# The first RMS norm of a hybrid decoder step moved into the first projection's block, and the squares of all four norms added on VectorE

## The reference

```
def rmsnorm(x, g):
    xf = xf * lax.rsqrt(jnp.mean(xf * xf, axis=-1, keepdims=True) + NORM_EPS)
    return xf * g

h = rmsnorm(x, norm_mix); z = h @ w_in           # then attention and RWKV branches on z
x = x + mixed @ w_out
h = rmsnorm(x, norm_mlp); x = x + square(relu(h @ w_ff1)) @ w_ff2
h = rmsnorm(x, norm_ple); x = x + sigmoid(h @ w_ple_gate) * (p @ w_ple)
y = rmsnorm(x, norm_final)
```

## Time and profile before

| | |
|---|---|
| time, median of 3 runs | 3305.36 us (3301.95 to 3306.35) |
| the profiled execution's own time | 3305.41 us |
| its span, first to last instruction | 3303.6 us |
| TensorE busy | 2969.5 us (90%) |
| VectorE busy | 1090.3 us (33%) |
| ScalarE busy | 954.6 us (29%) |
| mean granted TensorE clock | 0.935 |

### The profile page before, as it was taken

One profiled execution on the slowest core, in us unless ns is written; L12 is line 12 of the kernel. 1 busy time (PEld: TensorE's weight loads), 2 busy tenths in 40 slices (PEclk: granted clock), 3 DMA queues, 4 the chain that ended last, 5 costly groups with the idle time before them and its releaser, 6 DMA issues. The chain is left out here.

```text
span 3303.6 us, 62866 instructions
## 1 busy us (share of the span) xinstructions
PE 2969.5 (90%) x27318; PEld 2390.3 (72%) x27318; DVE 1090.3 (33%) x2430; ACT 954.6 (29%) x1797; POOL 407.5 (12%) x398
## 2 busy tenths in 40 slices
PE   6888797889999999999987999988999999999797
PEld 3666676856666666666655666687999999999785
DVE  1120202216777777777762111013111111111222
ACT  2120202025555555555542000013122221222212
POOL 0000001002111111112110000011221212212010
PEclk8889796599999999999988999999999999999898
DMA  3211102210001001001001110020111111111011
GB/s 135 80 61 58 70 14 78 105 27 23 25 11 33 19 17 33 19 17 33 13 3 47 42 41 30 12 103 26 45 38 44 44 38 44 38 44 44 29 40 61
DMA packets 57474, 139.18 MB, mean 42 GB/s; under 512 B 5008, under 2 KB 37008, under 8 KB 52400
## 3 DMA queue, kind: packets, MB, share of 16 engines
q1 hardware_dynamic: 53376, 116.03, 10.4%
q10 hardware_dynamic: 3888, 20.05, 1.8%
HBM read 119.54 MB, written 16.54 MB: 41 GB/s over the span
## 5 line engine op out<-in xcount | busy, mean ns | idle before, releaser
L1535 PE MATMUL psum<-hT,rkv_w 128*64 128x256 f32 (+1 forms) x3072 | 412.3, 395 | 11.2 <-DMA rkv_w<-in_w_pair 9.9
L1535 PEld LDWEIGHTS psum<-hT,rkv_w 128*64 128x64 f32 x3072 | 213.0, 138 | 115.6 <-issue 31.3
L129 PE MATMUL psum<-hT,merge_w 128*128 128x352 f32 x768 | 232.3, 463 | 12.2 <-DMA merge_w<-in_w_mix 12.2
L1856 POOL TENSOR_TENSOR ff_w_low<-ff_raw,ff_w_high 128x1024 fp32r<-128x1024 f32 x64 | 157.2, 2457 | 678.1 <-ACT ff_w_high L1851 678.1
L129 PEld LDWEIGHTS psum<-hT,merge_w 128*128 128x128 f32 x768 | 147.3, 192 | 95.1 <-issue 15.2
L152 PE MATMUL psum<-ff_high,ff_w_high 128*128 128x352 f32 x768 | 173.4, 335 | 38.7 <-DVE ff_low L2155 38.7
L2158 DVE TENSOR_TENSOR rwkv_out<-rwkv_out,psum 128x1056 f32<-128x1056 f32 x64 | 80.3, 1254 | 321.3 <-PE psum L152 321.3
L152 PE MATMUL psum<-h_high,ff_w_high 128*128 128x352 f32 x768 | 167.7, 327 | 12.9 <-DVE h_low L226 12.5
L152 PE MATMUL psum<-ff_low,ff_w_high 128*128 128x352 f32 x768 | 170.5, 332 | 0.0
L152 PE MATMUL psum<-ff_high,ff_w_low 128*128 128x352 f32 x768 | 170.0, 330 | 0.0
L1851 ACT ACTIVATE ff_w_high<-ff_raw 128x1024 fp32r<-128x1024 f32 x64 | 67.3, 1052 | 347.7 <-PE psum L152 347.7
(11 more groups left out here) (315 smaller groups left out, 5244.1 us busy)
## 6 DMA issues: line engine op xcount, KB each, us to landing
ff_raw<-in_w_ff SPq DMA_DIRECT2D x64, 512.0 KB, 3.5
merge_w<-in_w_mix SPq DMA_DIRECT2D x8, 1664.0 KB, 6.9
rkv_w<-in_w_pair SPq DMA_DIRECT2D x24, 512.0 KB, 4.1
rwkv_out<-in_kc ACTq DMA_DIRECT2D x4, 2048.0 KB, 12.9
ple_w<-in_w_ple SPq DMA_DIRECT2D x8, 640.0 KB, 3.8
x_in<-in_xT SPq DMA_DIRECT2D x2, 2112.0 KB, 10.8
rwkv_out<-in_xT ACTq DMA_DIRECT2D x1, 4224.0 KB, 13.5
out_yT<-y SPq DMA_DIRECT2D x8, 528.0 KB, 3.1
```

The source lines that it names most:

```text
L129: last = nc.tensor.matmul(acc[:, n, 0:TT], w[:, k, :], x[:, k, n * TT:(n + 1) * TT], start=k == 0, stop=k == kt - 1)
L1535: mm = nc.tensor.matmul(ahead[half[a], 0:width(v)], w3[:, k, n * P + a * C:n * P + a * C + C], hT[:, k, cols(v)], start=k == 0, stop=k == ...
L1856: return nc.gpsimd.tensor_tensor(parts[1][:, s, :], raw[:, s, 0:KT * P], parts[0][:, s, :].bitcast(F32), ALU.subtract)
```

## The change

It does two things.

The first norm loses its block. Its parts for ScalarE, TensorE and VectorE run ahead of the projection's own instructions in the block of `attention_projection` for the first group; the first product waits tile by tile for the normed input (`ready`), as the later stages do. One block issues all seven loads, the weights behind the second half of the input. The input now lies in `mixer` (the tile `rwkv_out`, which is free at that time) and not in a tile `x_in`. The two small operations on `mu1` and `ka1` move behind the attention stage, in the same block of their own.

In all four norms the squares are added on VectorE: the first square goes to a new tile `total`, and VectorE adds the other seven to it one after the other (`added`). TensorE multiplies `total` by the ones, three products (six passes) and no longer twenty-four (48 passes). ScalarE's squares wait for the add that freed their buffer (from the fourth on).

```
-def product(nc, acc, w, x, kt, width=None):
+def product(nc, acc, w, x, kt, ready=lambda k: None):
     for k in range(kt):
+        ready(k)
...
-            if k >= 2:
-                act.wait_ge(self.summed, k - 1)
-            nc.scalar.activation(self.sq[:, k % 2, :], self.x[:, k, :], ACT.Square).then_inc(self.squared, 1)
-        act.wait_ge(self.summed, KT)
+            if k >= 3:
+                act.wait_ge(self.added, k - 2)
+            nc.scalar.activation(self.sq[:, k % 2, :] if k else self.total[:, :], self.x[:, k, :], ACT.Square).then_inc(self.squared, 1)
+        act.wait_ge(self.summed, 1)
...
-        for k in range(KT):
-            pe.wait_ge(self.squared, k + 1)
-            for n in range(NT):
-                last = self.nc.tensor.matmul(self.psum[:, n, 0:TT], ones, self.sq[:, k % 2, n * TT:(n + 1) * TT], start=k == 0, stop=k == KT - 1)
-            last.then_inc(self.summed, 1)
+        pe.wait_ge(self.added, KT - 1)
+        for n in range(NT):
+            last = self.nc.tensor.matmul(self.psum[:, n, 0:TT], ones, self.total[:, n * TT:(n + 1) * TT], start=True, stop=True)
+        last.then_inc(self.summed, 1)
...
+        for k in range(1, KT):
+            vec.wait_ge(self.squared, k + 1)
+            if k > 1:
+                vec.wait_ge(self.added, k - 1)
+            nc.vector.tensor_tensor(self.total[:, :], self.total[:, :], self.sq[:, k % 2, :], ALU.add).then_inc(self.added, 1)
         vec.wait_ge(self.root, 2)
...
-        with nc.sbuf_tensor("x_in", [P, KT, T], F32) as x_in:
...
-            rms_norm(nc, "mix", x_in, gain("norm_mix"), cst_sb, hT, psum, ctx, arrive=(halves, tables_in))
...
+        x_in, tables_in, halves = mixer, sem("tables_in"), [sem(f"x_in{i}") for i in range(2)]
...
-                start_loads(nc, weights(0) + [(att_sb[:, :], ins["att_consts"], att_loaded)])
+                start_loads(nc, [(x_in[:, 0:KT // 2, :], ins["xT"][:, 0:KT // 2, :], halves[0]), (vec_sb[:, :], ins["vecs"], tables_in), (cst_sb[:, :], ins["consts"], tables_in),
+                                 (x_in[:, KT // 2:KT, :], ins["xT"][:, KT // 2:KT, :], halves[1]), *weights(0), (att_sb[:, :], ins["att_consts"], att_loaded)])
...
+                        norm = RmsNorm(nc, "mix", x_in, gain("norm_mix"), cst_sb, hT, psum, c3, ctx) if g == 0 else None
```

More of the change, by code:

```diff
@@ L174, in __init__ @@
         self.nc, self.x, self.gain, self.cst, self.out, self.low, self.psum = nc, x, gain, cst, out, low, psum
-        self.sq, self.rinv = sb("sq", 2, T), sb("rinv", T)
-        self.squared, self.summed, self.root, self.normed = (sem(n) for n in ("squared", "summed", "root", "normed"))
+        self.sq, self.total, self.rinv = sb("sq", 2, T), sb("total", T), sb("rinv", T)
+        self.squared, self.added, self.summed, self.root, self.normed = (sem(n) for n in ("squared", "added", "summed", "root", "normed"))
         if low is not None:
@@ L271, in dilated, with attention_projection @@
     return rows[:, bass.ds(first, 1), lo:lo + n].rearrange("p a b -> p (a b)")
-def attention_projection(nc, top, g, hT, wa, wb, wa_in, wb_in, tables_in, psum, qT, kT, vtok, vnew, k_out, v_out, prefetch):
+def attention_projection(nc, top, g, hT, wa, wb, wa_in, wb_in, tables_in, psum, qT, kT, vtok, vnew, k_out, v_out, prefetch, norm=None, arrive=None):
     with ExitStack() as ctx:
@@ L296, in _ @@
                 wv = wb[:, KT * P:].rearrange("p (k c) -> p k c", k=KT)
+                if norm is not None:
+                    pe.wait_ge(arrive[1], 32)
+                    norm.tensor(pe)
                 pe.wait_ge(wa_in, 16 * g + 16)
@@ L303, in _ @@
                     w = wk[:, :, i * P:(i + 1) * P] if i < 3 else wk1
-                    product(nc, psum[:, 3 * (i % 2):3 * (i % 2) + 3, :], w, hT, KT).then_inc(full, 1)
+                    product(nc, psum[:, 3 * (i % 2):3 * (i % 2) + 3, :], w, hT, KT, (lambda k: norm.ready(pe, k)) if norm is not None and i == 0 else (lambda k: None)).then_inc(full, 1)
                 for b in range(NB + 1):
@@ L318, in _ @@
             def _(act):
+                if norm is not None:
+                    norm.scalar(act, arrive)
                 for i in range(4):
@@ L325, in _ @@
             def _(vec):
+                if norm is not None:
+                    vec.wait_ge(arrive[1], 32)
+                    norm.vector(vec)
                 for b in range(NB + 1):
@@ L2180, in program @@
         gain = lambda n: vec_sb[:, VEC[n]:VEC[n] + KT]
-        with nc.sbuf_tensor("x_in", [P, KT, T], F32) as x_in:
-            tables_in, halves = sem("tables_in"), [sem(f"x_in{i}") for i in range(2)]
-            start_loads(nc, [(x_in[:, 0:KT // 2, :], ins["xT"][:, 0:KT // 2, :], halves[0]), (vec_sb[:, :], ins["vecs"], tables_in),
-                             (cst_sb[:, :], ins["consts"], tables_in), (x_in[:, KT // 2:KT, :], ins["xT"][:, KT // 2:KT, :], halves[1])])
-            rms_norm(nc, "mix", x_in, gain("norm_mix"), cst_sb, hT, psum, ctx, arrive=(halves, tables_in))
[L2187 to L2193, removed]
+        x_in, tables_in, halves = mixer, sem("tables_in"), [sem(f"x_in{i}") for i in range(2)]
         with ExitStack() as c1:
@@ L2223, in program @@
                     values = [(V[g][:, :, :, :], ins[f"vc{g}"], v_in)] if g < GROUPS - 1 else []
-                    attention_projection(nc, ctx, g, hT, wa, wb, wa_in, wb_in, att_loaded, psum, qT, kT, vtok, vnew, outs["k_all"][g], outs["v_all"][g], values)
+                    with ExitStack() as c3:
+                        norm = RmsNorm(nc, "mix", x_in, gain("norm_mix"), cst_sb, hT, psum, c3, ctx) if g == 0 else None
+                        attention_projection(nc, ctx, g, hT, wa, wb, wa_in, wb_in, att_loaded, psum, qT, kT, vtok, vnew, outs["k_all"][g], outs["v_all"][g], values, norm, (halves, tables_in))
                     attention_prompt(nc, ctx, g, counts, psum, qT, kT, vtok, att, cst("ident"), scratch, ahead)
@@ L2230, in program, with _ @@
             load_all(nc, sem("vnew_stored"), [(outs["v_new"], vnew[:, :, :])])
+        derived = sem("derived")
+        with nc.Block() as block:
+            @block.vector
+            def _(vec):
+                nc.vector.tensor_scalar(mu1[:, :], vec_sb[:, VEC["shift_mu"]:VEC["shift_mu"] + RT], -1.0, 1.0, ALU.mult, ALU.add).then_inc(derived, 1)
+                nc.vector.tensor_scalar(ka1[:, :], vec_sb[:, VEC["k_a"]:VEC["k_a"] + KT], -1.0, 1.0, ALU.mult, ALU.add).then_inc(derived, 1)
         with ExitStack() as c2:
```

## The result

The changed kernel takes 3276.69 us, the median of 4 runs (3274.63 to 3277.29), against 3303.65 for the kernel before in its 4 runs (3301.15 to 3306.35): 27.0 us faster, a ratio of 0.9917 with a 95% interval of 0.99 to 0.9934. The forecast was 3283, a range of 3277 to 3291. The time lies 0.3 us outside that range, on the side of the greater gain.

What follows compares the result with a forecast made beforehand. TensorE, busy 90% of the span, was taken as the bound, with gains where it waits around the norms. 16.6 (start) + 6.5 (later norms) - 0.6 (moved block) = 22.5 us, so 3305.4 became 3283 us, range 3277 to 3291.

Steps and rivals of the forecast that it cites:

- The chain that it told: First norm: input squared, adds, six passes, logarithm, normed tiles, projection; later norms: two squares, seven adds, six passes, logarithm; chance 0.76.
- The projection: First product with w_qk: starts at 31.5 or 31.6 us instead of 48.18, 16.6 us earlier.
- the first logarithm: First norm: starts at 26.45 us instead of 27.47, 1.0 us earlier.
- The later norms' chain: mlp, ple and final, first square to logarithm: 15.1 us each, gaining 0.5, 2.8 and 3.2, together 6.5 us.
- the add's pitch: VectorE's seven dependent adds per norm: starts 1.29 us apart, with 1.24 and 1.40 as bounds.
- The flush: Rival: each VectorE add waits for its predecessor's flush, pitch 2.24 us, leaving 2.5 us gain, 3303 us; chance 0.03.
- The moved block: Small block of mu1 and ka1, now behind the attention stage: charged 0.6 us, range 0 to 0.9.
- the rival of the shared queue: Start: loads share the queue's rate, so the input's second half lands 10.7 us later; 3294 us; chance 0.06.
- the last term of the range: Whole kernel: runs of one kernel lie 4.4 us apart, so 2 us either way, giving 3277 to 3288.
- One sign that the prediction had named for being wrong: Stretch from the projection to mlp: the forecast is wrong if it no longer has its old length.
- its slower rival: Attention stages: moved forward, TensorE's clock spends more time at half; 60 us more gives 3313 us; chance 0.03.

Runs made afterwards that it cites:

- e5: The kernel before, unchanged, run and profiled a second time: 3303.01 us, ratio 1.0003.
- e6: The changed kernel, unchanged, run more often and profiled a second time: 3281.07 us, ratio 0.9928 against the kernel before.
- e4: Two useless VectorE adds, some 1.65 us, ahead of the first norm's normed tiles in the changed kernel: 3282.33 us, 0.9937 of the kernel before.
- e7: The same two useless VectorE adds, some 1.65 us, ahead of the first norm's normed tiles in the kernel before: 3304.49 us, ratio 1.0004.

## Why the prediction was wrong, and where it was right

The chain that it told is the chain of the trace. The projection starts 16.4 us earlier (16.6 forecast), with the first logarithm at 26.72 (26.45). The later norms' chain takes 15.51 (15.1), so that they give 5.4 and not 6.5: the add's pitch is 1.36 and not 1.29, nearer to the 1.40 of the earlier trace rows; it is a dependent add, and that row was the one with a dependent add. The flush that the Trainium skill's page "VectorE: DVE Perf Modes", section "The DRAIN you can't avoid", puts behind an operation is not seen between the adds: 1.36 between starts leaves 0.1 us to a 1.26 us add. The moved block cost 0.6, as charged. The weights did not delay the input (16.21 against 16.2), so the rival of the shared queue is out. In sum 21.1 of the forecast 22.5 us. Between the second profiles, e5 and e6, the start alone gives 17.6 (49.22 and 31.64), so that the path is 22.4 there; the start of the kernel before has a scatter of its own, of about 1 us.

The step that failed is the last term of the range: "runs of one kernel lie 4.4 us apart, 2 us either way", which was taken from three runs. On one chip 23 runs of the kernel before went from 3294.4 to 3313.7, 19 us, and its medians were 3303.65, 3305.93, 3303.37 and 3305.14 in the four comparisons. Of the 6.3 us between the forecast and the measured time 1.8 are this alone, 3305.4 against 3303.65; the other 4.5 are a gain of 27.0 in place of 22.5. The changed kernel's four runs of the first comparison lie between 3274.6 and 3277.3, four of the five of the second between 3280.7 and 3282.0. The two intervals overlap, and 3283 / 3305.4 = 0.9932 lies in both. No stage shows the 4.5 us as an effect of the change: e5 and e6 show the attention stage at 82.0 and 85.3 in the kernel before, at 82.0 and 85.8 in the changed one, and the stretch up to `mlp` has the same mean in ten profiles. That all of it is scatter is not shown. Over all runs the means of the two kernels (64 runs and 9) lie 26.0 us apart, by an estimate from their scatter 2 us either way if the chips are alike, and the paths of the two pairs of profiles are 21.1 and 22.4.

One sign that the prediction had named for being wrong came true: the stretch from the projection to `mlp` lost its old length. But it came true with nothing changed as well (2216.4 and 2209.3 in the kernel before), so it could not tell a cost of the change from scatter. The forecast named the mechanism itself, in its slower rival, and dismissed it by the same three runs; it can go either way, and it should have widened the range on both sides.

What sets the scatter is shown as far as this: TensorE's clock stands at half in stretches that lie elsewhere in each execution, in stages where it waits in short steps; more of it makes these stages longer, and useless products that keep it from falling make them shorter. Here are the same 8 us of the first attention group, 18 to 26 us behind the store of the values, in the two profiles of the kernel before, its first and e5:

```profile
157.00:165.00 8.00, 6.70 (x25) 6.05 (x25) 1.71 (x3) 3.10 (x9) 0.00 (x0) 0.58 0.05 18
157.94:165.94 8.00, 5.51 (x41) 5.00 (x40) 4.16 (x5) 4.28 (x11) 0.80 (x2) 1.00 0.07 24
```

At a clock of 0.58 TensorE gets through some 25 passes in them, at 1.00 through 41. Over the 23 runs of the kernel before, the slower a run, the lower its mean clock, with few exceptions. In the nine runs of the changed kernel the mean clock tells little: 3274.63 us came at 0.934, 3281.98 at 0.935. The Trainium skill says of the clock ("TensorE: Matmul & The Clock Gate", "Part 1: The HAM clock gate") that the default is the slow state, which activity releases, and that the point of the change varies from run to run. The two profiles agree with the second: 0.58 and 1.00 in the lines above. What decides where the stretches fall in one execution stays open: nothing here controls it, and e4 and e7, shifted by 1.6 us, did not show it in their times. Nor can it be said whether the mean gain is nearer to 21 or to 26 us.

## What to carry to other kernels

Before putting a range around a gain of under 1%, look how long the stages that the change doesn't touch are in two profiles of one kernel; three times of a kernel are too few for its scatter. A wait that one engine has for weights is best read together with the block ends ahead of their issue: loads that depend on nothing belong in the first block, behind what is needed first. And where TensorE waits in steps of about a microsecond, its half clock may cost more than some products that nobody needs.

## What was not expected of the hardware

Three useless products in each of 24 waits made a kernel that was bound by TensorE faster by 13.5 us of 3305. And one kernel, unchanged, on one chip, took from 3294 to 3314 us, with a mean granted clock of 0.940 in the fastest run and 0.932 in the slowest.
